# The opening of a hybrid decoder layer: first weight units one k tile at a time, x piece 0 on another queue, a longer warm-up

## The reference

```python
proj = jnp.einsum('bsd,dc->bsc', x, w_in[l])        # 256x2048 by 2048x6144
q_a, k_a, v_a, q_b, k_b, v_b = jnp.split(proj, splits, axis=-1)
...                                                 # rope, attention, subln
attn_out = jnp.einsum('bsc,cd->bsd', mix, w_out[l])
x = layer_norm(DEEPNORM_ALPHA * x + attn_out, ln1_g[l], ln1_b[l])
hdn = jnp.square(jax.nn.relu(jnp.einsum('bsd,df->bsf', x, w_ff1[l])))
ff_out = jnp.einsum('bsf,fd->bsd', hdn, w_ff2[l])
x = layer_norm(DEEPNORM_ALPHA * x + ff_out, ln2_g[l], ln2_b[l])
```

## Time and profile before

| | us |
|---|---|
| median of 3 runs | 1123.57 |
| lowest, highest | 1123.15, 1124.5 |
| the profiled execution: time | 1124.69 |
| the profiled execution: span in the trace | 1122.7 |
| PE busy in the span | 1108.8 (99%) |
| DVE, ACT busy | 646.6 (58%), 499.5 (44%) |
| DMA | 215.50 MB, mean 192 GB/s |

### The profile page before, as it was taken

How to read it: one execution, slowest core, us unless ns; L and a number is a source line. 1 busy time by engine, 2 the same in 40 slices (tenths; PEclk the granted TensorE clock), 3 DMA queues, 4 the chain that set the end, 5 groups by cost and what they waited for, 6 DMA issues and landing times.

```text
span 1122.7 us, 14718 instructions
## 1 busy us (share of the span) xinstructions
PE 1108.8 (99%) x5500; PEld 932.5 (83%) x5500; DVE 646.6 (58%) x673; ACT 499.5 (44%) x632; POOL 27.0 (2%) x53
## 2 busy tenths in 40 slices
PE   8999999999999999999999999999999999999996
PEld 7888888888888878888888888888888888888885
DVE  4656756646556685565556556655445445445446
ACT  4445565654454524444444444444433433433331
POOL 1000100000000020000000000000000000000001
PEclk9999999999999999999999999999999999999998
DMA  8755455575545855666666666667555556556572
GB/s 253 251 169 183 154 169 169 154 259 169 169 156 168 281 173 165 187 185 197 192 189 184 190 188 188 185 195 270 189 193 198 189 192 198 190 193 198 190 266 89
DMA packets 109481, 215.50 MB, mean 192 GB/s; under 512 B 6720, under 2 KB 9152, under 8 KB 108800
## 3 DMA queue, kind: packets, MB, share of 16 engines
q1 hardware_dynamic: 108064, 207.71, 58.1%
q0 software_dynamic: 1376, 7.21, 1.9%
HBM read 210.70 MB, written 4.19 MB: 191 GB/s over the span
## 4 chain that ended last, share of the span: by engine, by line
PE 97%; DVE 1%; DMA 1%; issue 0%; POOL 0%; SPq 0%; POOLq 0%; ACT 0%; DVEq 0%
PE low_ps L375 11%; PE low_ps L379 11%; PE low_ps L377 11%; PE low_ps L578 11%; PE high_ps L377 10%; PE high_ps L375 10%; PE high_ps L379 10%; PE high_ps L578 9%; PE low_ps L583 5%; PE high_ps L583 5%; PE high_ps L434 1%; PE high_ps L459 1%; PE high_ps L420 1%; DMA y<-in_x 1%; PE high_ps L443 0%; PE high_ps L350 0%
## 5 line engine op out<-in xcount | busy, mean ns | idle before, releaser
L858 DVE TENSOR_TENSOR w_lo<-w_raw,w_hi 128x1024 fp32r<-128x1024 f32 x376 | 459.3, 1223 | 405.4 <-ACT w_hi L644 404.8
L644 ACT ACTIVATE w_hi<-w_raw 128x1024 fp32r<-128x1024 f32 x376 | 398.3, 1059 | 518.8 <-PE high_ps L379 195.6
L375 PE MATMUL high_ps<-w_hi,hidT_hi 128*128 128x512 f32 x480 | 186.7, 389 | 0.0
L377 PE MATMUL high_ps<-w_lo,hidT_hi 128*128 128x512 f32 x480 | 186.7, 389 | 0.0
L379 PE MATMUL high_ps<-w_hi,hidT_lo 128*128 128x512 f32 x480 | 186.7, 389 | 0.0
L578 PE MATMUL low_ps<-x1T,w_hi 128*128 128x512 f32 x512 | 176.7, 393 | 0.0
L375 PE MATMUL low_ps<-w_hi,xT_hi 128*128 128x512 f32 x384 | 155.7, 405 | 0.0
L578 PE MATMUL high_ps<-x1T,w_hi 128*128 128x512 f32 x448 | 155.0, 394 | 0.0
L379 PE MATMUL low_ps<-w_hi,xT_lo 128*128 128x512 f32 x384 | 150.8, 393 | 0.0
L377 PE MATMUL low_ps<-w_lo,xT_hi 128*128 128x512 f32 x384 | 150.4, 392 | 0.0
L583 PE MATMUL low_ps<-x1T,w_lo 128*128 128x256 f32 x512 | 136.9, 278 | 0.0
(11 more groups left out here) (135 smaller groups left out, 804.1 us busy)
## 6 DMA issues: line engine op xcount, KB each, us to landing
w_raw<-in_w_ff SPq DMA_DIRECT2D x252, 512.0 KB, 3.6
w_raw<-in_w_in SPq DMA_DIRECT2D x96, 512.0 KB, 3.9
w_raw<-in_w_out SPq DMA_DIRECT2D x32, 512.0 KB, 3.8
y<-in_x SPq DMA_DIRECT2D x8, 256.0 KB, 6.2
side_raw<-in_w_ff SPq DMA_DIRECT2D x4, 512.0 KB, 6.8
ln_spill<-y POOLq DMA_DIRECT2D x8, 256.0 KB, 2.8
y<-ln_spill POOLq DMA_DIRECT2D x1, 2048.0 KB, 10.4
ln_gb<-in_ln_g POOLq DMA_DIRECT2D x1, 1024.0 KB, 6.3
```

The costliest lines, as they stand in the source:

```text
L375: pe.matmul(acc[:, tt, 0:cols], hi[:, toks], right_hi[:, slot, w], start=(t == 0), stop=False)
L377: pe.matmul(acc[:, tt, 0:cols], hi[:, toks], right_lo[:, slot, w], start=False, stop=False)
L644: act.activation(w_hi[:, slot, :], w_raw[:, slot, :], ACT.Copy).then_inc(w_rounded, units)
L858: dve.tensor_tensor(w_lo[:, slot, :], w_raw[:, slot, :], w_hi[:, slot, :].bitcast(F32), ALU.subtract).then_inc(w_split, units)
```

## The change

- SP no longer loads the identity. ACT's queue starts it and x piece 0 before ACT's first rounding.
- Units 0 to 3 are loaded, rounded and split in two halves of one k tile, each half with semaphores of its own (`half_loaded`, `half_rounded`, `half_split`). PE starts a k tile when its half is there.
- x runs one piece ahead: piece 0 is turned alone at the start; piece k + 1 is turned inside unit k after its first three matmuls (units 0 to 3), or before unit k's products (units 4 to 6).
- `WARM_UP` is 7 at the start and 8 after the turning of piece 0; none later.
- POOL waits for five used units ahead of the load of `tables`.

```diff
-WARM_UP = (6, 2, 2)
+WARM_UP = (7, 8)
...
         for k in range(UPH):
-            cols = slice(k * KU * P, (k + 1) * KU * P)
-            sp.dma_start(y1[:, :, cols], x_d[:, :, cols]).then_inc(x_loaded[k], 16)
-            load_chunk_unit(sp, w_in_d, k, k, in_chunk(0), k % SLOTS)
+            if k:
+                load_x(sp, k)
+            if k < SLOTS:
+                for kk, loaded in enumerate((half_loaded[k], w_loaded[k])):
+                    sp.dma_start(w_raw[:, k, kk * NC:(kk + 1) * NC],
+                                 w_in_d[:, k, kk, in_chunk(0), :]).then_inc(loaded, 16)
+            else:
+                load_chunk_unit(sp, w_in_d, k, k, in_chunk(0), k % SLOTS)
...
+        def first_unit(k):
+            pe.wait_ge(turn_split, k + 1)
+            for kk in range(KU):
+                pe.wait_ge((half_split, w_split)[kk], k + 1)
+                for tt in range(TT):
+                    toks, cols = slice(tt * P, (tt + 1) * P), slice(kk * NC, (kk + 1) * NC)
+                    hi, lo = xT_hi[:, KU * k + kk, toks], xT_lo[:, KU * k + kk, toks]
+                    acc = proj_ps[0][:, tt, :]
+                    pe.matmul(acc, hi, w_hi[:, k, cols], start=(k == 0 and kk == 0), stop=False)
+                    pe.matmul(acc, hi, w_lo[:, k, cols], start=False, stop=False)
+                    ins = pe.matmul(acc, lo, w_hi[:, k, cols], start=False, stop=False)
+                    if kk == 0 and tt == 0:
+                        transpose_x(k + 1)
+            ins.then_inc(w_used, 1)
...
             if i == 0:
-                for x in {0: (0, 1), 1: (2, 3)}.get(k, (k + 2,)):
-                    if x < UPH:
-                        transpose_x(x)
-                    if x < 2:
-                        warm_up(WARM_UP[x + 1])
+                if k < SLOTS:
+                    first_unit(k)
+                    return
+                if k + 1 < UPH:
+                    transpose_x(k + 1)
                 pe.wait_ge(turn_split, k + 1)
...
         warm_up(WARM_UP[0])
         pe.wait_ge(ident_loaded, 16)
+        transpose_x(0)
+        warm_up(WARM_UP[1])
...
+        act.dma_start(ident_t[:, :], table[:, 0:P]).then_inc(ident_loaded, 16)
+        load_x(act, 0)
         for k in range(SLOTS):
             round_x(k)
-            round_unit(k, k, 1)
+            for kk, (loaded, rounded) in enumerate(((half_loaded[k], half_rounded),
+                                                    (w_loaded[k], w_rounded))):
+                cols = slice(kk * NC, (kk + 1) * NC)
+                act.wait_ge(loaded, 16)
+                act.activation(w_hi[:, k, cols], w_raw[:, k, cols], ACT.Copy).then_inc(rounded, 1)
...
             split_x(k)
-            split_unit(k, k)
+            for kk, (rounded, split) in enumerate(((half_rounded, half_split),
+                                                   (w_rounded, w_split))):
+                cols = slice(kk * NC, (kk + 1) * NC)
+                dve.wait_ge(rounded, k + 1)
+                dve.tensor_tensor(w_lo[:, k, cols], w_raw[:, k, cols], w_hi[:, k, cols].bitcast(F32),
+                                  ALU.subtract).then_inc(split, 1)
...
+        pool.wait_ge(w_used, 5)
         pool.dma_start(tables[:, :], table[:, P:T_COLS]).then_inc(tables_loaded, 16)
...
-            sp.dma_start(ident_t[:, :], table[:, 0:P]).then_inc(ident_loaded, 16)
```

More of the change, by code:

```diff
@@ L227, in hybrid_layer @@
     side_rounded, side_split = sem("side_rounded"), sem("side_split")
+    half_loaded = [sem(f"half_loaded{k}") for k in range(SLOTS)]
+    half_rounded, half_split = sem("half_rounded"), sem("half_split")
     w_rounded, w_split, w_used = sem("w_rounded"), sem("w_split"), sem("w_used")
@@ L284, in load_chunk_unit, with load_x @@
         sp.dma_start(dst, src).then_inc(w_loaded[slot], 16)
+    def load_x(queue, k):
+        cols = slice(k * KU * P, (k + 1) * KU * P)
+        queue.dma_start(y1[:, :, cols], x_d[:, :, cols]).then_inc(x_loaded[k], 16)
     def sync_program(sp):
         for k in range(UPH):
-            cols = slice(k * KU * P, (k + 1) * KU * P)
-            sp.dma_start(y1[:, :, cols], x_d[:, :, cols]).then_inc(x_loaded[k], 16)
-            load_chunk_unit(sp, w_in_d, k, k, in_chunk(0), k % SLOTS)
+            if k:
[6 more added lines that the diff above has]
+                load_chunk_unit(sp, w_in_d, k, k, in_chunk(0), k % SLOTS)
         for u in range(UPH, U_OUT):
```

## The result

| | before | changed |
|---|---|---|
| median of 14 runs each | 1123.36 us | 1125.34 us |
| lowest, highest | 1121.44, 1124.5 | 1123.83, 1126.05 |
| ratio of the times | | 1.0017 (95% interval 1.001 to 1.0024) |
| the profiled execution: time, span | 1124.69, 1122.7 | 1124.15, 1122.0 |

The change costs 2.0 us. By the bound of 0.2% (2.25 us) that is still no change, and it lies inside the range, 0.1 us under its upper end; but the interval leaves out 1, and the forecast was 1123.6. The two profiled executions alone would say the opposite: that of before (1124.69) lies above all 14 times of its kernel here, that of the changed kernel (1124.15) is the fourth lowest of its own.

A forecast was written before the change was run, and what follows sets the result against it. PE's own queue from the first product on was taken to bound the kernel; 0.9 us won at unit 0's end minus 0.9 lost in waits gave no change, 1123.6 us, range 1121.2 to 1125.4.

The forecast's parts named there:

- an earlier end of unit 0: Opening: unit 0's products end at 13.5 us, against 14.37 before; 0.9 us won.
- waits from running one piece ahead: Units 1 to 7: PE waits 0.2 us over units 1 to 3, 0.4 at 4, 0.2 at 7; 0.9 lost (0.6 to 1.0).
- The tables: POOL's later load: issued about 27.0, landed at 38.3, before the first rope at 39.27; hidden by 1.0 us, costing nothing.
- the halves: Units 0 to 3: halved loads, roundings and splits add four instructions each on SP, ACT and DVE; cost nothing.
- T: Start of turning x piece 0 in the opening: 4.8 us, bounds 4.6 and 5.9; first product at T + 4.78.
- rival 2: Opening: piece 0 shares DMA engines with unit 0, lands at 5.9; 1124.7 us, or 1126.1 with a late clock; chance 0.14.
- the clock: Opening: TensorE goes from 1.2 to 2.4 GHz 6.0 us after PE's last idle stretch, at 10.8 us.
- rival 1: Opening: clock rises at 7.1, unit 0 ends at 11.75; 2.6 to 3.3 us won before stalls, 1121.2 to 1121.9; chance 0.28.

The follow-up runs named there:

- the kernel with the weights ahead of x: Changed kernel, x still one piece ahead, but ACT and DVE take weights of units 1 to 7 before the x piece; median 1122.27 us, ratio 0.9987 to 1.0005.
- the tables-later kernel: Kernel before with only POOL's wait for five used units added ahead of the tables load; median 1123.13 us, mean 0.0 against before.

## Why the prediction was right or wrong

**Right: the scale and what bounds it.** The time is PE's queue from the first product on, and the change stayed under 0.2%. The two terms that the forecast named, an earlier end of unit 0 against waits from running one piece ahead, are the two that decide. The tables came out as said, and the halves as nearly free: two of them take 1.14 us on ACT and 1.28 on DVE, a whole unit 1.05 and 1.22. That the time lies inside the range is in part luck: the middle of the forecast missed by 1.7 us, and the upper part of the range, put there for a late piece 0, took up a loss of which 1.1 us came from waits that were summed too small.

**Wrong: the sum of the waits, 0.9 for 2.0 us.** This is the main miss. The chain was the right one, the sizes were not. For units 1 to 3 I had the split ready 3.24 us after the unit's start and PE done at 3.21, and gave 0.07 for the hand-over. In the trace the turning starts 0.76 after the unit's start (9.12 - 8.36), not 0.68, because after a wait PE's first matmul is slower (0.30 to the next, 8.36 to 8.66, against 0.23), and PE starts 0.14 after the split's end (11.00 + 0.69 to 11.83). So each of units 1 to 3 pays 0.26 (3.47 for 3.21) and not 0.07. Unit 4 pays about 0.8 for 0.4 (4.35 after unit 3, against 3.56 in the kernel with the weights ahead of x) and unit 7 about 0.4 for 0.2: 2.0 in all, and undone in either of two ways it was 2.0 us. Where a step is forecast to be ready just when it is needed, these two small delays are the term.

**Wrong: T, the start of turning piece 0, 4.8 for 5.6 to 6.2.** I took the lower end of 4.6 to 5.9, with the argument that the first half of unit 0 can cost the piece at most some 0.65 us. From ACT's queue piece 0 landed 4.3 to 4.9 us after its issue (five traces), from the front of SP's 2.7 to 3.8 (eight). It came behind both halves of unit 0, not one: they were started 0.46 and 0.03 us ahead of it and landed 3.2 and 3.7 after their issue. From 4.0 to 4.5 us ACT's queue moved 0.14 MB and SP's 0.05, so the two did share the time; but ACT's queue moved its first packet only after 2.5 us, SP's from 1.5 on, and how much of the delay is the sharing and how much the queue itself no run shows. The Trainium skill ("DMA: Bandwidth & Descriptors", Issuing engines are not separate DMA queues) says that such loads interleave on the same engines; the trace agrees, as both queues moved packets in that half microsecond. So the late landing of rival 2 happened, if not quite at 5.9. It cost 1.2 us in the mean, as much as the turning moves between the two profiled executions (5.63 to 4.45).

**Partly wrong: the clock.** I let the rise come 6.0 us after PE's last idle stretch, in both kernels. In the changed kernel's profiled execution the passes ran at 2.4 GHz from 6.1 us on, right after an idle gap of 1.2 us, so rival 1's early rise happened without its condition, even sooner than its 7.1, and unit 0 ended at 11.63 where rival 1 had 11.75. It did not win: the waits were 2.0 us and not 0.9, and the median of before was not that of its profiled execution (next point). In another execution of the same kernel part of the same passes ran slow. What the forecast had right is that much of the spread between executions is the clock's, 1.06 of the 1.6 us between the changed kernel's two profiled ones; the kernel with shorter gaps (before, warm-ups 7, 4, 2) is within 1.3 us in 11 runs where the kernel before is spread over 3.4 in 33. The Trainium skill ("TensorE: Matmul & The Clock Gate", Part 1) says that the number of slow matmuls at the start varies from run to run; the traces agree, with ten of unit 0's twelve products slow in that of before and three, the third in part, in that of the tables-later kernel, whose opening is the same.

**A baseline read from one execution.** The profiled execution of before was 1.7 us over its median of 1123.0. I counted unit 0's end at 14.37 as the kernel's, while another profiled execution with the same opening (the tables-later kernel, 1123.13) reaches it at 12.64. A gain against the late end of a spread is not a gain against the median. The shares that the runs gave are 2.0 for the waits, 1.2 for the late piece 0 and 1.2 won by halves and warm-ups together: 2.0 + 1.2 - 1.2 = 2.0, against 1.8 to 2.0 measured. So in the mean unit 0 ends when it did before: the last two cancel, where I had 0.9 won, and the waits are left as the whole difference.

## What to carry to other kernels

An order in which something is prepared is a queue on every engine that it passes: when the late item (here a turned piece) stands ahead of the ready one (weights already landed), moving its production later delays both, and swapping two entries in the queues gives the same 2 us as producing it earlier. A load that the first step waits for belongs at the front, ahead of all others: started from a second queue at the same moment as others, it landed later here, by 1.2 us between the two traces. Where a few us at the start depend on the clock, look at several executions before taking one profile as the base, and try a few more warm-up passes first: six of them, in short idle gaps of PE, gave 1.0 us here.

## What the runs showed of the hardware

- Two queues at the start: the identity (64 KB) took 3.4 to 3.6 us from issue to landing on ACT's queue beside SP's loads and 1.8 to 2.0 at the front of SP's; a 256 KB piece behind it 4.3 to 4.9 and 2.7 to 3.8.
- Warm-up on zeros alone can bring the clock up: after 14 passes from 1.05 to 4.4 us, an idle gap of 1.2 us and one turning the next passes took 0.12 us each. It does so in part of the executions only: in the other profiled one of the same kernel sixteen passes took 3.16 us and not 1.95.
- Six more passes in PE's opening, which shortened idle gaps of 0.73 and 1.23 us to 0.52 and 0.39, gave 1.0 us in the mean. The low end of the times stayed, the high end went.
- The granted clock in the profile's rows reads 1.00 from 0 to 16 us in before and in the changed kernel, although products stood 0.43 us apart until 13.9 in the first. In these openings the clock had to be read from the distance between matmuls.
- The 768 KB of tables landed 11.3 us after an issue at 21.7 us and 6.1 to 7.8 after one behind unit 4 (24.8 to 28.1 us, in eleven traces), and in none of the thirteen did PE wait between unit 8 and 60 us.
